# The half-head exchange of the rotation in two attention layers: fp32 matmuls against on-chip transfers

## The reference, cut to what matters

```python
h = rms_norm(x, g_mix[layer])                       # 512 tokens x 1024
proj = einsum('bsd,dc->bsc', h, w_in[layer])
qa, ka, va, iq, ik, iw, qb, kb, vb = split(proj, ...)
# qa, ka, qb, kb: heads of 64; iq (8 heads) and ik (one): heads of 32

def apply_rope(x, cos, sin):
    half = x.shape[-1] // 2
    x1, x2 = x[..., :half], x[..., half:]
    return concatenate([x1 * c - x2 * s, x2 * c + x1 * s], axis=-1)
```

## Time and profile before

| | |
|---|---|
| median of three runs | 3061.12 us |
| profiled execution, first to last instruction (span) | 3050.0 us |
| PE (TensorE) busy | 2809.9 us, 92% |
| DVE (VectorE) busy | 1782.9 us, 58% |
| ACT (ScalarE) busy | 1134.1 us, 37% |
| projection stage of the layers | about 1618 to 1796 us and 2335 to 2513 us |

### The profile page before, as it was taken

One profiled execution on the slowest core, in us unless ns is written; L12 is line 12 of the kernel. 1 busy time (PEld: TensorE's weight loads), 2 busy tenths in 40 slices (PEclk: granted clock), 3 DMA queues, 4 the chain that ended last, 5 costly groups with the idle time before them and its releaser, 6 DMA issues.

```text
span 3050.0 us, 41699 instructions
## 1 busy us (share of the span) xinstructions
PE 2809.9 (92%) x16794; PEld 2123.9 (70%) x16794; DVE 1782.9 (58%) x3266; ACT 1134.1 (37%) x2028; POOL 145.4 (5%) x139
## 2 busy tenths in 40 slices
PE   7998977888999999999988987999999996999998
PEld 4887755775666666666636755788887774778887
DVE  4257866665767777767655787433334679443333
ACT  3323233222155555556513336422222326432222
POOL 0000000000012222212100000000000000000000
PEclk9998888989999999999999989999999998999999
DMA  6210002414278989999882210324223210222412
GB/s 224 83 56 21 1 1 64 126 49 152 88 268 340 345 343 354 358 357 347 339 325 97 83 35 1 118 61 140 70 76 117 83 56 8 84 69 77 138 52 73
DMA packets 180782, 433.08 MB, mean 142 GB/s; under 512 B 20131, under 2 KB 109542, under 8 KB 161254
## 3 DMA queue, kind: packets, MB, share of 16 engines
q1 hardware_dynamic: 161862, 396.72, 36.3%
q0 software_dynamic: 18720, 33.60, 2.9%
HBM read 426.56 MB, written 38.29 MB: 152 GB/s over the span
## 4 chain that ended last, share of the span: by engine, by line
PE 67%; DVE 9%; DMA 5%; ACT 3%; issue 2%; POOL 0%; SPq 0%; POOLq 0%; DVEq 0%; ACTq 0%
PE ps L298 15%; PE ps L300 15%; PE ps L299 15%; PE ps L2498 6%; DMA hg<-h_rows,idx 2%; PE ps L2014 2%; PE ps L1506 2%; DMA ring<-in_ew 2%; PE ps L2524 1%; DVE Pb L3418 1%; PE ps L2737 1%; PE ps L3139 1%; PE ps L2218 1%; DVE bi L3240 1%; DMA yr<-y_rows 1%
## 5 line engine op out<-in xcount | busy, mean ns | idle before, releaser
L2939 DVE TENSOR_TENSOR wf<-ring,wf 128x1024 fp32r<-128x1024 f32 (+1 forms) x152 | 181.5, 1196 | 316.8 <-ACT wf L2935 316.8
L2935 ACT ACTIVATE wf<-ring 128x1024 fp32r<-128x1024 f32 (+1 forms) x152 | 156.7, 1033 | 349.2 <-PE ps L300 349.2
L298 PE MATMUL ps<-hxh,wf 128*128 128x512 f32 x704 | 276.2, 392 | 2.8 <-DVE hxl L3084 2.8
L299 PE MATMUL ps<-hxl,wf 128*128 128x512 f32 x704 | 275.8, 392 | 0.0
L300 PE MATMUL ps<-hxh,wf 128*128 128x512 f32 x704 | 275.8, 392 | 0.0
L2436 DVE TENSOR_TENSOR spA<-ring,spA 128x1024 fp32r<-128x1024 f32 x156 | 184.3, 1221 | 105.6 <-ACT spA L2431 105.3
L2498 PE MATMUL ps<-ring,hdT 128*128 128x512 f32 x520 | 234.8, 594 | 0.8 <-issue 0.8
L2431 ACT ACTIVATE spA<-ring 128x1024 fp32r<-128x1024 f32 x156 | 157.3, 1053 | 54.9 <-DMA ring<-in_ew 48.6
L2436 DVE TENSOR_TENSOR spB<-ring,spB 128x1024 fp32r<-128x1024 f32 x104 | 124.0, 1220 | 65.8 <-ACT spB L2431 65.6
L2498 PEld LDWEIGHTS ps<-ring,hdT 128*128 128x128 f32 x520 | 93.8, 190 | 94.3 <-issue 90.4
L298 PEld LDWEIGHTS ps<-hxh,wf 128*128 128x128 f32 x704 | 133.5, 190 | 31.5 <-DVE hxl L3084 3.6
(11 more groups left out here) (615 smaller groups left out, 6196.8 us busy)
## 6 DMA issues: line engine op xcount, KB each, us to landing
ring<-in_ew SPq DMA_DIRECT2D x65, 2048.0 KB, 12.4
ring<-in_ew SPq DMA_DIRECT2D x65, 1024.0 KB
ring<-in_w_in SPq DMA_DIRECT2D x17, 2048.0 KB, 7.8
ring<-in_w_gate SPq DMA_DIRECT2D x20, 1024.0 KB, 5.5
ring<-in_w_up SPq DMA_DIRECT2D x20, 1024.0 KB, 8.0
ring<-in_w_down SPq DMA_DIRECT2D x16, 1024.0 KB, 5.0
adaw<-in_ada_w SPq DMA_DIRECT2D x24, 512.0 KB, 6.3
ring<-in_w_out SPq DMA_DIRECT2D x6, 2048.0 KB, 7.9
```

The source lines that it names most:

```text
L298: pe.matmul(o, lhs[0], rhs[0], start=start, stop=False)
L299: pe.matmul(o, lhs[0], rhs[1], start=False, stop=False)
L2935: act.activation(item_part(n)[0], item_raw(n), ACT.Copy).then_inc(*w_hi.inc(n))
L2939: v.tensor_tensor(item_part(n)[1], item_raw(n), f(item_part(n)[0]), ALU.subtract).then_inc(*w_lo.inc(n))
```

## The change

The columns of the weights of the rotated blocks are reordered when the inputs are laid out, so that the two partners of a rotation stand in neighbouring columns (pairs). The exchange of halves so becomes an exchange of neighbouring partitions. The tables of cosine and sine follow that order. For 18 of the 19 blocks of each layer the matmul is gone. ScalarE, after its copy into r1, waits for the copy's own signal and issues two transfers from on-chip memory to on-chip memory: the odd partitions of r1 go to the even ones of r2, and the even to the odd, 64 rows of 2 KB each. Two semaphores in turn count them, and VectorE waits for both transfers of its block before the second product, which now reads r2 and not PSUM. Block 2 keeps its transposes and its two matmuls, now in index_key, which TensorE runs behind step 3 as before. TensorE's waits for p_ro and p_v ahead of the exchange go with it.

```diff
-    m["sw64"] = (s // 64 == t // 64) & ((s % 64 + 32) % 64 == t % 64)
-    m["sw32"] = (s // 32 == t // 32) & ((s % 32 + 16) % 32 == t % 32)
-    m["rsw32"] = (s < 32) & ((t % 32 + 16) % 32 == s)
+    m["rsw32"] = (s < 32) & (t % 32 == s + 1 - 2 * (s % 2))
...
-        out.append(c[p % half])
-        out.append(np.where((p < half)[:, None], -s[p % half], s[p % half]))
+        out.append(c[p // 2])
+        out.append(np.where((p % 2 == 0)[:, None], -s[p // 2], s[p // 2]))
...
+    def swap_dma(act, l, c):
+        act.wait_ge(*p_r.val((l, c)))
+        for q in range(2):
+            act.dma_start(r2[q:128:2, c % 2, :], r1[1 - q:128:2, c % 2, :]).then_inc(*d_sw.inc(SWAPS.index((l, c))))
...
-    p_sw = Signal(sem("rope_swap"), [(l, n) for l in range(2) for n in range(19)])
+    p_sw = Signal(sem("rope_swap"), range(2))
+    SWAPS = [(l, n) for l in range(2) for n in range(19) if n != 2]
+    d_sw = Loads([sem(f"d_swap{k}") for k in range(2)], [2] * len(SWAPS))
...
-        def swap(c):
-            pe.wait_ge(*p_r.val((l, c)))
-            if c >= 2:
-                pe.wait_ge(*p_ro.val((l, c - 2)))
-            if c == 2:
...
-            if c in (3, 4):
-                pe.wait_ge(*p_v.val((l, 1, 2 + c % 2)))
-            sw = C("rsw32") if c == 2 else C("sw32") if c < 2 else C("sw64")
-            pe.matmul(ps[2 + c % 2][:, :], sw, r1[:, c % 2, :]).then_inc(*p_sw.inc((l, c)))
+        def index_key():
+            pe.wait_ge(*p_r.val((l, 2)))
+            for i in range(4):
+                pe.transpose(ps[0][:, i * 128:(i + 1) * 128], r1[:, 0, i * 128:(i + 1) * 128], ident)
+            pe.matmul(ps[1][:, :], C("rep32"), r1[:, 0, :])
+            pe.matmul(ps[2][:, :], C("rsw32"), r1[:, 0, :]).then_inc(*p_sw.inc(l))
...
-            if 1 <= p <= 3:
-                swap(p - 1)
-            elif p >= 12:
-                swap(p - 9)
+            if p == 3:
+                index_key()
...
-        swap(18)
...
                 act.activation(r1[:, c % 2, :], ps[c % 2][:, :], ACT.Copy).then_inc(*p_r.inc((l, c)))
+                if c != 2:
+                    swap_dma(act, l, c)
...
-            v.wait_ge(*p_sw.val((l, c)))
-            v.tensor_tensor(r2[:, c % 2, :], ps[2 + c % 2][:, :], rope[:, t + 1, :], ALU.mult).then_inc(*V.inc())
+            if c != 2:
+                v.wait_ge(*d_sw.val(SWAPS.index((l, c))))
+            v.tensor_tensor(r2[:, c % 2, :], ps[2][:, :] if c == 2 else r2[:, c % 2, :], rope[:, t + 1, :], ALU.mult).then_inc(*V.inc())
...
+    def pairs(x, dim):
+        return x.reshape(2, 1024, -1, 2, dim // 2).swapaxes(3, 4).reshape(x.shape)
```

More of the change, by code:

```diff
@@ L3125, in lproj_pe @@
         n0 = first_of[l, "in"]
-        def swap(c):
-            pe.wait_ge(*p_r.val((l, c)))
-            if c >= 2:
-                pe.wait_ge(*p_ro.val((l, c - 2)))
-            if c == 2:
-                for i in range(4):
-                    pe.transpose(ps[0][:, i * 128:(i + 1) * 128], r1[:, 0, i * 128:(i + 1) * 128], ident)
-                pe.matmul(ps[1][:, :], C("rep32"), r1[:, 0, :])
-            if c in (3, 4):
-                pe.wait_ge(*p_v.val((l, 1, 2 + c % 2)))
-            sw = C("rsw32") if c == 2 else C("sw32") if c < 2 else C("sw64")
-            pe.matmul(ps[2 + c % 2][:, :], sw, r1[:, c % 2, :]).then_inc(*p_sw.inc((l, c)))
+        def index_key():
[4 more added lines that the diff above has]
+            pe.matmul(ps[2][:, :], C("rsw32"), r1[:, 0, :]).then_inc(*p_sw.inc(l))
         def index(g):
@@ L3275, in rope_part @@
             if c == 2:
-                v.wait_ge(*p_sw.val((l, c)))
+                v.wait_ge(*p_sw.val(l))
                 v.tensor_scalar(iw[:, :, :], v4(ps[0])[:, :, 32:40], float(32 ** -0.5 * 8 ** -0.5), None, ALU.mult).then_inc(*V.inc())
             v.tensor_tensor(dst, ps[1][:, :] if c == 2 else r1[:, c % 2, :], rope[:, t, :], ALU.mult).then_inc(*V.inc())
-            v.wait_ge(*p_sw.val((l, c)))
-            v.tensor_tensor(r2[:, c % 2, :], ps[2 + c % 2][:, :], rope[:, t + 1, :], ALU.mult).then_inc(*V.inc())
+            if c != 2:
+                v.wait_ge(*d_sw.val(SWAPS.index((l, c))))
+            v.tensor_tensor(r2[:, c % 2, :], ps[2][:, :] if c == 2 else r2[:, c % 2, :], rope[:, t + 1, :], ALU.mult).then_inc(*V.inc())
             v.wait_ge(*V.val())
@@ L3799, in _layout @@
     W = a["w_in_2"]
-    w_in_2 = np.concatenate([W[:, :, 0:1024], W[:, :, 1832:2856], W[:, :, 1536:1832], np.zeros_like(W[:, :, 0:88]),
-                             W[:, :, 1024:1536], W[:, :, 2856:3368]], 2)
+    def pairs(x, dim):
+        return x.reshape(2, 1024, -1, 2, dim // 2).swapaxes(3, 4).reshape(x.shape)
+    w_in_2 = np.concatenate([pairs(W[:, :, 0:1024], 64), pairs(W[:, :, 1832:2856], 64), pairs(W[:, :, 1536:1824], 32), W[:, :, 1824:1832],
+                             np.zeros_like(W[:, :, 0:88]), W[:, :, 1024:1536], W[:, :, 2856:3368]], 2)
     out = {
```

## The result

The changed kernel took 3035.02 us in the median of four runs (3023.85 to 3036.64) against 3061.59 us for the kernel before beside it; the ratio is 0.9912, interval [0.9898, 0.9927]. Run once more over six runs it gave 3030.1 us against 3060.77 us, ratio 0.9895 [0.9875, 0.9915]. The forecast was 3033.7 us, which lies between the two medians of the same kernel.

The account below looks back on a forecast made before the run. TensorE, without idle time in the projection stage, was taken as the bound; -28.6 us for its exchanges and +1.2 for the tails gave -27.4, so 3061.1 became 3033.7 us, range 3028 to 3044.

Parts of the forecast that it names:

- TensorE is the bound and its time is given back: Projection steps: TensorE never idles, so 17 exchanges a layer at 0.84 us save 14.3 us a layer, 28.6 for both.
- ScalarE's issues hidden: Projection steps: two issues a block at 0.46 us each fit into 1.7 us of slack and cost nothing.
- VectorE as full as TensorE, but fitting: Steps with two search rounds: VectorE's turn needs 5.44 us against the new step of 5.62, costing nothing.
- Transfers hidden inside the steps: Projection steps: transfers land 2.3 us after issue, early enough that TensorE does not stall.
- addition of about 1 us: Transfers beside weight loads: landing assumed about 1 us later, hidden by the 7.5 us allowed.
- the 7.5 at which I set the limit: Transfers inside the steps: data may land as late as 7.5 us after the issue before TensorE stalls.
- The tail: Block 18's rotation after the last step: grows by 0.6 us a layer, 1.2 in all, and can't hide.
- B: Rival: transfers queue behind weight loads, landing 10.1 us after issue; 21 us lost, about 3055 us; chance 7%.
- C: Rival: landing always slow, 5 to 7 us; hidden in steps, tail grows 4.3 us a layer, 3041 us; chance 8%.
- D: Rival: ScalarE's issues become the bound; at 2.2 us an issue 33 us slower, 3094 us; chance 6%.
- E: Rival: the exchange is hidden anyway, its 0.86 us filled by something else; no gain, 3061 + 1; chance 3%.
- My sign of error: Attention stage: a length change of more than 1 us would show the forecast wrong.

Follow-up runs that it names:

- pe_back: Changed kernel plus an unread fp32 matmul of the same size on TensorE for each of the 36 blocks, transfers kept: 3060.6 us, ratio to before 1.0000.
- iss4: Changed kernel with four transfers of 32 rows for each block in place of two of 64: 3038.1 us, ratio to before 0.9929.
- no_dma: Changed kernel without the 72 transfers and VectorE's waits for them: 3029.86 us, ratio to before 0.9889.
- dve_plus: Changed kernel with VectorE making the first product of each rotation twice: 3043.56 us, ratio to before 0.9948.
- iss8: Changed kernel with eight transfers of 16 rows for each block in place of two of 64: 3100.24 us, ratio to before 1.0139.
- load2: Changed kernel with a 2 MB side copy issued behind each of six weight loads of a layer: 3036.97 us, ratio to before 0.9921.
- again: Changed kernel as it is, run and traced once more: 3030.1 us, ratio to before 0.9895.

## Why the prediction was right

- **TensorE is the bound and its time is given back: right**, shown by pe_back, which gives the time back, and by TensorE's waits ahead of line 3139. The size was 14.3 us a layer and is 13.8. The failed piece is my count: I put 17 exchanges inside the row of steps, "blocks 3 to 17 behind steps 12 to 26". The one behind step 26 stands after the last step's end E, in the tail, whose 4.24 us already held it. It is 16, at the chain's 0.86 us and not the 0.84 I took: 16 x 0.86 = 13.8. The two errors partly cancel; 0.5 us a layer, 1.1 in all (28.6 against 27.5), is left.
- **ScalarE's issues hidden: right, with less room than I gave.** I took 0.46 us an issue; it is 0.56 in the median, and the split starts 1.85 us after the copy, not 1.5. The slack for more was about 1.1 us (iss4). And "costs nothing" holds for the steps only: by no_dma the issues lengthen each tail by 0.9 us.
- **VectorE as full as TensorE, but fitting: right.** Four turns in a row (from 1724.55 us) took 5.45, 5.46, 6.03 and 5.44 us, the third (1741.49 - 1735.46) with its 0.49 of waiting; I had forecast 5.44. dve_plus shows the edge.
- **Transfers hidden inside the steps: right** (no_dma), but my "addition of about 1 us" beside a load was too small: 2.9 to 4.9 us, landings of up to 6.9 against the 7.5 at which I set the limit. I had bounded it by 10.1, and the truth lies in the middle. That it stayed under the limit, by 0.6 us, was luck as far as my 1 us goes.
- **The tail: 0.6 us forecast, 0.5 measured.** It comes as said: block 18's first product at 1.5 us and not 1.2 after the last step, landing 2.1 instead of 2.3 us. That the tail "can't hide" is not shown (no_dma).
- **Rivals.** B does not come even with twice the bytes. C is refuted by 2.0 to 2.1 us. D has the right mechanism and too high a price: I let each us beyond the limit lengthen every step by itself, but the path runs over two steps (iss8: 1.1 us in a plain step where that rule gives 2.25, 1.7 in the mean of all). By the path over two steps alone its break-even would have been at 0.84 x 2 = 1.7 us beyond the limit, not at 0.84; that is an estimate, and no run stands there. E is refuted by the steps, 169.0 to 155.2 us and back with pe_back.
- **My sign of error** "the attention stage itself changes its length by more than 1 us" did show, 2.4 and 3.3 us, and is no sign: the stage behind the last rotation differs by as much between traces with the same attention code, 543.9 (load2) to 546.9 us (again) in layer 0 and 532.9 (again) to 536.8 us (first trace) in layer 1.
- Sum by the measured terms: -27.5 + 0.9 = -26.6 us, which is the difference of the medians in the first comparison. In the second that difference is 30.7 us. No stage in the traces accounts for the 4 us more, so an agreement to 0.1 us is luck; what is shown is a sum within the spread of the runs.

## What to carry to other kernels

Work taken from the engine that is busy without a gap comes back one for one, if what replaces it fits into the other engines' idle time within one period; so add up each engine's turn, and look for the path that crosses periods: what goes over is shared among the periods that it spans, here two, unless another limit comes first. When counting what stands "inside" a loop, put each instance on one side of the boundary at which the tail begins. A small transfer that lands after 2 us alone took up to three times that here when a big load ran beside it, so the wait for it needs that much room. And work put on an engine with slack can be free inside the loop and still show where the loop ends, as the issues do in the tail.

## What the runs showed that I had not expected

The first issue of a pair on ScalarE takes 0.47 us and the second 0.61, for 64 rows each; with transfers of 16 rows the first takes 0.51 and each further one 0.61. So the count matters, not the size (eight take 5.00 us). A transfer on its own queue lands after 4.9 to 7.5 us whether 2 or 4 MB stand in the other queue. In the whole program the time up to the first copy of these layers, with the same code up to there, ranged from 1626.4 to 1640.6 us over eleven traces, more than half of the whole gain: a single span can't price a change of 1%.
